# Causal linear attention in a decoder trunk: the scores and outputs of the four heads multiplied head by head instead of two heads at a time

## What is computed

```python
# chunks of 64 tokens; dk = 48, dv = 96, 4 heads
q_dec = q * jnp.exp(bcum)
k_inv = k * jnp.exp(-bcum)
scores = jnp.einsum("bnihd,bnjhd->bnhij", q_dec, k_inv)
scores = jnp.where(causal, scores, 0.0)
o_intra = jnp.einsum("bnhij,bnjhe->bnihe", scores, v)
u = jnp.einsum("bnchd,bnche->bnhde", k_tail, v)
# scan over chunks: state[n+1] = decay[n] * state[n] + u[n]
o_inter = jnp.einsum("bnihd,bnhde->bnihe", q_dec, s_prev)
return (o_intra + o_inter)
```

## Time and profile before

| | |
|---|---|
| median of three runs | 2295.99 us (2295.87 to 2296.01) |
| profiled execution | 2295.87 us |
| its span in the trace | 2294.1 us |
| PE busy | 2210.2 us, 96% of the span |
| DVE, ACT, POOL busy | 1067.6, 803.9, 1029.6 us |
| granted TensorE clock, mean | 0.99 |

### The profile page before, as it was taken

One profiled execution on the slowest core, in us unless ns is written; L12 is line 12 of the kernel. 1 busy time (PEld: TensorE's weight loads), 2 busy tenths in 40 slices (PEclk: granted clock), 3 DMA queues, 4 the chain that ended last, 5 costly groups with the idle time before them and its releaser, 6 DMA issues.

```text
span 2294.1 us, 25940 instructions
## 1 busy us (share of the span) xinstructions
PE 2210.2 (96%) x10680; PEld 1840.1 (80%) x10680; DVE 1067.6 (47%) x1109; ACT 803.9 (35%) x1098; POOL 1029.6 (45%) x430
## 2 busy tenths in 40 slices
PE   7999999998999899999999999999988998999997
PEld 6888888786788788888878888888767887888886
DVE  2333235887735533333343332368776364333334
ACT  2322224636543422222233222246455434222223
POOL 5444445434552544444454444454256435444442
PEclk9999999999999999999999999999999999999999
DMA  4333321322341233333233233222124322333321
GB/s 167 98 95 100 115 90 57 99 79 78 105 125 56 67 99 97 96 113 101 72 94 101 92 108 101 94 65 92 60 90 121 106 65 65 101 95 99 113 96 50
DMA packets 55718, 213.20 MB, mean 93 GB/s; under 512 B 6064, under 2 KB 8368, under 8 KB 55344
## 3 DMA queue, kind: packets, MB, share of 16 engines
q1 hardware_dynamic: 54304, 207.64, 28.4%
q10 hardware_dynamic: 1296, 3.90, 0.5%
HBM read 209.42 MB, written 2.10 MB: 92 GB/s over the span
## 4 chain that ended last, share of the span: by engine, by line
PE 86%; DVE 6%; ACT 3%; ACTq 1%; POOL 1%; DVEq 1%; issue 1%; DMA 0%; SPq 0%
PE psum L467 25%; PE psum L468 24%; PE psum L471 24%; PE psum L503 2%; POOL w_lo L390 1%; PE psum L599 1%; PE psum L483 1%; PE psum L507 1%; DVE x L1444 1%; ACT x L1054 1%; DVE psum L1549 1%; ACT w_hi L1016 1%; PE psum L444 1%; PE psum L489 1%; ACT act_hi L1069 1%
## 5 line engine op out<-in xcount | busy, mean ns | idle before, releaser
L390 POOL TENSOR_TENSOR w_lo<-raw,w_hi 128x1024 fp32r<-128x1024 f32 (+3 forms) x360 | 945.1, 2627 | 1203.8 <-ACT w_hi L1016 1203.7
L1016 ACT ACTIVATE w_hi<-raw 128x1024 fp32r<-128x1024 f32 (+3 forms) x360 | 405.6, 1127 | 1326.5 <-PE psum L471 1205.3
L467 PE MATMUL psum<-act_hi,w_hi 128*128 128x512 f32 (+1 forms) x1836 | 719.2, 392 | 3.6 <-ACT w_hi L1016 3.2
L468 PE MATMUL psum<-act_lo,w_hi 128*128 128x512 f32 (+1 forms) x1836 | 715.0, 389 | 0.0
L471 PE MATMUL psum<-act_hi,w_lo 128*128 128x512 f32 (+1 forms) x1836 | 453.8, 389 | 0.0
L467 PEld LDWEIGHTS psum<-act_hi,w_hi 128*128 128x128 f32 (+1 forms) x1836 | 344.7, 188 | 80.2 <-DVE x L1386 3.0
L468 PEld LDWEIGHTS psum<-act_lo,w_hi 128*128 128x128 f32 (+1 forms) x1836 | 344.7, 188 | 72.5 <-issue 1.4
L471 PEld LDWEIGHTS psum<-act_hi,w_lo 128*128 128x128 f32 (+1 forms) x1836 | 344.7, 188 | 72.0
L1469 DVE TENSOR_TENSOR work<-work,psum 128x512 f32<-128x512 f32 x88 | 60.5, 688 | 610.8 <-PE psum L471 561.9
L1474 DVE TENSOR_TENSOR h_lo<-work,h_hi 128x512 fp32r<-128x512 f32 x88 | 237.5, 2699 | 6.6
L467 PE MATMUL psum<-h_hi,w_hi 128*128 128x512 f32 x616 | 239.6, 389 | 0.0
(11 more groups left out here) (247 smaller groups left out, 2248.5 us busy)
## 6 DMA issues: line engine op xcount, KB each, us to landing
raw<-w_in SPq DMA_DIRECT2D x176, 512.0 KB, 3.5
raw<-w_out SPq DMA_DIRECT2D x64, 704.0 KB, 4.0
raw<-w_mix SPq DMA_DIRECT2D x36, 512.0 KB, 3.5
raw<-w_kv SPq DMA_DIRECT2D x32, 512.0 KB, 3.5
raw<-w_mixout SPq DMA_DIRECT2D x16, 576.0 KB, 3.8
raw<-w_q SPq DMA_DIRECT2D x16, 512.0 KB, 4.2
raw<-w_o SPq DMA_DIRECT2D x16, 512.0 KB, 3.5
raw<-w_v SPq DMA_DIRECT2D x4, 768.0 KB, 4.2
```

The lines of the kernel that those rows point to most:

```text
L390: nc.gpsimd.tensor_tensor(w_lo[:, n % SPLIT, 0:width], raw[:, n % RAW, 0:width], w_hi[:, n % SPLIT, 0:width].bitcast(F32), ALU.subtract).t ...
L467: nc.tensor.matmul(o, hi, b_hi, start=start and k == 0, stop=False)
L468: nc.tensor.matmul(o, hi, b_lo, start=False, stop=False)
L1016: A(w_hi[:, n % SPLIT, 0:width], raw[:, n % RAW, 0:width], ACT.Copy).then_inc(w_hi_made, 1)
```

## The change

The functions scores and output of the PE stream take a head h instead of a pair g. Each multiplies all four token tiles for one head and signals once for that head; the calls scores(0), scores(1) take the place of the old scores(0), and so on. The same matmuls run with the same operands into the same banks. The loop order changes: the matmuls of the two heads of a pair, which alternated, now come one head after the other. The waits become those of the head: from head 2 on, scores(h) waits for the mask of head h - 2, and output(h) for ACT's reading of head h - 2. The functions of the other engines are as before.

```diff
--- before.py
+++ after.py
@@ -763,41 +763,35 @@
                                 start=True, stop=True)
                     last.then_inc(u_ready, 1)
 
-                def scores(g):
-
-                    if g:
-                        pe.wait_ge(score_masked, layer * HEADS + 2)
+                def scores(h):
+
+                    if h >= 2:
+                        pe.wait_ge(score_masked, layer * HEADS + h - 1)
+                    g, r0 = h // 2, h % 2 * CHUNK
                     for t in range(TT):
                         cols = slice(t * P, (t + 1) * P)
-                        for r in range(2):
-                            r0 = r * CHUNK
-                            last = nc.tensor.matmul(psum[:, 4 + r, cols],
-                                                    KI[g][r0:r0 + CHUNK, cols],
-                                                    QQ[g][r0:r0 + CHUNK, cols],
-                                                    start=True, stop=True)
-                    last.then_inc(score_ready, 2)
-
-                def output(g):
-                    if g == 0:
+                        last = nc.tensor.matmul(psum[:, 4 + h % 2, cols], KI[g][r0:r0 + CHUNK, cols],
+                                                QQ[g][r0:r0 + CHUNK, cols], start=True, stop=True)
+                    last.then_inc(score_ready, 1)
+
+                def output(h):
+                    if h == 0:
                         pe.wait_ge(state_ready, layer * (NCHUNK - 1) + NCHUNK - 1)
-                    else:
-                        pe.wait_ge(o_read, layer * HEADS + 2)
+                    if h >= 2:
+                        pe.wait_ge(o_read, layer * HEADS + h - 1)
+                    g, r0 = h // 2, h % 2 * CHUNK
                     for t in range(TT):
-                        for r in range(2):
-                            h = 2 * g + r
-                            nc.tensor.matmul(psum[0:DV, 6 + r, t * P:(t + 1) * P],
-                                             v_tok[:, t, h * DV:(h + 1) * DV],
-                                             SC[h][:, t * P:(t + 1) * P], start=True, stop=False)
+                        nc.tensor.matmul(psum[0:DV, 6 + h % 2, t * P:(t + 1) * P],
+                                         v_tok[:, t, h * DV:(h + 1) * DV],
+                                         SC[h][:, t * P:(t + 1) * P], start=True, stop=False)
                         for n in (2 * t, 2 * t + 1):
                             if n:
                                 cols = slice(n * CHUNK, (n + 1) * CHUNK)
-                                for r in range(2):
-                                    r0 = r * CHUNK
-                                    last = nc.tensor.matmul(psum[0:DV, 6 + r, cols],
-                                                            state[r0:r0 + CHUNK, n, g, :],
-                                                            QQ[g][r0:r0 + CHUNK, cols],
-                                                            start=False, stop=n % 2 == 1)
-                    last.then_inc(o_ready, 2)
+                                last = nc.tensor.matmul(psum[0:DV, 6 + h % 2, cols],
+                                                        state[r0:r0 + CHUNK, n, g, :],
+                                                        QQ[g][r0:r0 + CHUNK, cols],
+                                                        start=False, stop=n % 2 == 1)
+                    last.then_inc(o_ready, 1)
 
                 def group_norm(t, source, ready, signal):
 
@@ -832,8 +826,10 @@
                 project("g", 1)
                 turned_keys()
                 scores(0)
+                scores(1)
                 project("g", 2)
-                scores(1)
+                scores(2)
+                scores(3)
                 update(0)
                 update(1)
                 project("g", 3)
@@ -841,10 +837,12 @@
                     update(n)
                 project("ya", 0)
                 output(0)
+                output(1)
                 project("ya", 1)
                 rms(0)
                 rms(1)
-                output(1)
+                output(2)
+                output(3)
                 group_norm(0, CC, conv_done, gn_mean)
                 project("ya", 2)
                 rms(2)
```

## The result

The changed kernel takes 2314.7 us (median of four runs, 2313.6 to 2319.3) against 2296.0 us before: the ratio is 1.0084, with a 95% interval of 1.0066 to 1.0101. It is 18.7 us slower. The forecast had 9.8 us, and its range ended at 2309.6. The profiled execution took 2316.6 us, of which its span is 2314.7; that this equals the median is chance.

The account below looks back on a forecast made before the run. The prediction took PE, busy 96% of the span, as the bound. From the profiled 2295.87 us, +9.8 for the outputs and +0.1 for the scores gave 2305.8 us, with a range of 2303.6 to 2309.6.

Parts of the forecast that it names:

- What bounds, and that nothing is hidden: PE bounds; time added ahead of group_norm(0) counts in full, since DVE's work and the end of PE's wait move with it.
- PE's hole: PE's 4.6 us wait for DVE's last tap before group_norm(1), claimed to keep its length and give no cover.
- the forecast's path: From PE's outputs through group_norm(0) to DVE's centered(0) and last tap, then back to PE for group_norm(1).
- Output, +9.8 us: PE's output matmuls: a pair takes 6.57 us against 4.12, 2.45 more, for two pairs in two layers.
- The pace of a lone stream: In outputs' half-array parts with one head: taken as 0.082 us per round; other paces gave +7.6 or +12.0 us.
- Scores, +0.1 us: PE's scores: the second head's calls overlap the first's, costing 0.02 us for each of four pairs.
- strict order: Rival on the scores: the second head's calls don't pass the first's waiting ones; 3.5 us on top, 2309.3 us, chance 0.18.
- no term here beyond some tenths: TensorE clock: the hole keeps its length and PE isn't idle in the new stretches, so almost no effect.
- The hole takes it up: Rival: PE's 4.6 us wait in each layer absorbs the outputs' delay; 2296.5 us, chance 0.04.
- not slower: Rival: PE runs the other head's half-array matmuls past waiting full-array ones in output; 2294.4 to 2296.0 us, chance 0.05.

Follow-up runs that it names:

- norm_early: Kernel before, with group_norm(0) moved ahead of the second output pair, directly behind rms(1); 2297.3 us, ratio 1.0006.
- scores_two_by_two: Kernel before, with the scores of a pair issued as two calls of the first head, two of the second, and so on; 2296.5 us, ratio 0.9999.
- scores_only: Kernel before, with only the scores going head by head as in the change, outputs as before; 2297.1 us, ratio 1.0004.
- outputs_only: Kernel before, with only the outputs going head by head as in the change, scores as before; 2314.0 us, ratio 1.0081.
- heads_full_twice: outputs_only with each full-array call of an output issued twice, the second replacing the first; 2311.5 us, ratio 1.0065.
- pairs_twice: Kernel before, two heads alternating, with each output pair computed twice over into the same banks; 2309.5 us, ratio 1.0060.
- lone_long: pairs_grouped with the odd heads' state matmuls left out and the even heads' added six times; 2331.3 us, ratio 1.0153.
- pairs_grouped: Kernel before, with a pair's eight full-array output calls first, then its fourteen half-array calls, two heads alternating; 2291.1 us, ratio 0.9978.
- heads_grouped: Changed kernel, with a head's four full-array output calls first and its seven half-array calls behind them; 2299.3 us, ratio 1.0013.

## Why the prediction was wrong, point by point

**What bounds, and that nothing is hidden: held, but for a second path.** DVE's wait for group_norm(0) grew from 9.0 to 17.8 us in layer 0 and 15.2 in layer 1, where the forecast had 13.9, and PE's hole stayed in layer 0 (4.6, 4.5) and shrank to 3.4 in layer 1. norm_early showed that DVE starts where the forecast said, and added what it had missed: a path of the same length through project ya 2 and ACT. In the changed kernel that one ended last in both layers. It also starts behind the outputs, so the conclusion that nothing is hidden stands, though not by the forecast's path alone.

**Output, +9.8 us: held.** At full clock a pair takes 6.53 us (forecast 6.57), 4 x 2.41 = 9.6 us. The half part kept its 0.48 with half the records. The pace of a lone stream, the declared unknown, was the row's.

**Scores, +0.1 us: mis-sized.** They took 0.55 us more per pair, 2.2 in all, between the forecast (0.02) and the rival of strict order (0.87). The updates, from which I had the 0.02, have two calls waiting for each half of the columns; the scores have four on one tile. The forecast named that difference, but priced only the whole of it, as a rival, and nothing between. scores_two_by_two (+0.10 us per pair) and scores_only (+0.55) show what lies between. The Trainium skill, "TensorE: Matmul & The Clock Gate", Part 3, The mechanism, has matmuls start and end in program order. Here 1.71 us is less than one after the other allows (1.90), and the second head's first record starts before three of the first head's, so the page's rule doesn't hold for these calls as the trace records them. It would have put the pair 0.2 to 0.3 us too high; my 0.02 put it 0.53 too low.

**The clock, "no term here beyond some tenths": this step failed.** It carries 8.4 us of the stages above, directly or through the waits behind a slow project ya 2, and outputs_only lies 8 us above its work. I had reasoned from the one fall in the rows of before, in the idle hole, that PE must be idle for the clock to fall, and that PE was not idle in the new stretches. The runs refute that. PE was busy without a gap and the clock still went to 1.2 GHz in stretches where its records used little of the array: one half at a time, with short full-array parts between. Twice the full-array work in between held it (heads_full_twice), two heads at a time held it for 8.3 us (pairs_twice), and one lone half-array stream without changes of shape lowered it (lone_long). These three together leave neither the length of the stretch, nor the changes of shape, nor the order by heads as the cause, and point to how little of the array is used. What in that use counts is not shown: a half that stands still, full-array calls that are too far apart, or short gaps between the records of a lone stream, which the profile can't show since it models where a matmul ends. Where the fall begins was not measured either.

**How it spreads.** The price is not paid in the outputs alone. Where the clock fell late in a pair, the projection behind it ran slow (5.58 to 6.90 us for project ya 1; 5.86 to 8.04 for project ya 2 of layer 1), with group_norm(0) between the pair and project ya 2, and the fall in the hole came on top of that. From trace to trace it strikes at other pairs: in the changed kernel it missed the first pair of layer 1, in outputs_only the second pair of layer 0.

**The rivals.** "The hole takes it up" and "not slower" got 0.09 together and didn't occur. "Strict order" was partly right on the scores, worth 2.2 of its 3.5 us. The clock stood among the rivals with "some tenths" and no chance, and it decided whether the range held.

## What to carry to other kernels

Calls on two halves of the array run together when they are issued near each other: keep them alternating, or at most two in a row, and put no full-array call between them. Each change between full-array and half-array calls cost about 0.16 us here, so group the calls by shape; that gave the one version faster than before (2291.1 us). When a change makes PE use less of its array at a time, price the clock as well: take a longer stretch at the lower clock as a rival with a number, even where PE shows no idle time. And before counting on a shorter path, look for the next one that ends within a microsecond of it, in ACT's and DVE's timelines.

## What the runs showed of the hardware

- The clock fell to 0.50 with PE busy in the whole of a window (lone_long: 12.60 of 12.60 us, mean clock 0.70), so PE's busy time does not tell whether it holds.
- Added full-array work (7.0 us) did not make a kernel slower, 2311.5 against 2314.0 us; the clock stayed at 1.00 in its output pairs (heads_full_twice, outputs_only).
- Half-array calls in a row on one half are passed by calls for the other half only in part: 1.16 us for sixteen records alternating, 1.26 two calls by two, 1.71 four by four.
- The first full-array call can open the accumulation for the whole bank and the later ones join without opening it anew (pairs_grouped, heads_grouped), so that all half-array calls can stand at the end; the sums are the same, and a pair takes 3.17 us in place of 4.12 (pairs_grouped).
